# Moving operands of the 256-token stages at one column, and transposes between the passes of the last two feed-forwards

## What is computed

```
h = x + 0.5 * swiglu(rmsnorm(x, ffn1_norm[l]), gate, up, down)   # 1024 -> 2816 -> 1024
u = rmsnorm(h, mix_norm[l])
h = h + (pool_mixer(u) if l == 0 else mla_attention(u, shared k and v))
h = h + 0.5 * swiglu(rmsnorm(h, ffn2_norm[l]), gate, up, down)
out = rmsnorm(h, final_norm)[:, 16:]

swiglu(h) = (silu(h @ w_gate) * (h @ w_up)) @ w_down
```

## Time and profile before

| | |
|---|---|
| median of three runs | 1222.82 us |
| profiled execution | 1223.91 us |
| its span | 1222.4 us |
| TensorE busy | 1201.7 us (98%), 9978 matmuls |
| VectorE busy | 859.5 us (70%) |
| ScalarE busy | 635.1 us (52%) |
| GpSimd busy | 174.1 us (14%) |

### The profile page before, as it was taken

One profiled execution on the slowest core, in us unless ns is written; L12 is line 12 of the kernel. 1 busy time (PEld: TensorE's weight loads), 2 busy tenths in 40 slices (PEclk: granted clock), 3 DMA queues, 4 the chain that ended last, 5 costly groups with the idle time before them and its releaser, 6 DMA issues.

```text
span 1222.4 us, 23818 instructions
## 1 busy us (share of the span) xinstructions
PE 1201.7 (98%) x9978; PEld 1179.0 (96%) x9978; DVE 859.5 (70%) x1215; ACT 635.1 (52%) x990; POOL 174.1 (14%) x178
## 2 busy tenths in 40 slices
PE   6999999999999999999999999999999999999998
PEld 4999989999999999999999999999999998999998
DVE  6789888776666866655766666667666787766653
ACT  5657646665445444543644444444545457645532
POOL 3025324000322000022200001230001231000021
PEclk9999999999999999999999999999999999999999
DMA  9897765757564555654355565456556532665550
GB/s 363 312 349 265 241 241 181 257 203 282 161 222 151 175 186 182 196 176 142 118 181 184 184 193 174 155 180 197 193 187 210 191 121 87 206 187 194 189 174 35
DMA packets 67051, 239.17 MB, mean 196 GB/s; under 512 B 7380, under 2 KB 8549, under 8 KB 66944
## 3 DMA queue, kind: packets, MB, share of 16 engines
q1 hardware_dynamic: 66144, 235.15, 57.9%
q0 software_dynamic: 656, 2.24, 0.5%
q10 hardware_dynamic: 144, 0.26, 0.1%
HBM read 236.55 MB, written 1.07 MB: 194 GB/s over the span
## 4 chain that ended last, share of the span: by engine, by line
PE 91%; DVE 3%; ACT 1%; issue 0%; DVEq 0%
PE G L636 27%; PE G L637 27%; PE G L638 27%; DVE sb_wlo L1624 1%; PE A L636 1%; PE A L637 1%; PE A L638 1%; PE A L788 0%; PE A L1082 0%; PE A L803 0%; PE A L776 0%; PE G L1137 0%; PE G L1138 0%; PE G L1139 0%; DVE sb_rstd L1672 0%
## 5 line engine op out<-in xcount | busy, mean ns | idle before, releaser
L1624 DVE TENSOR_TENSOR sb_wlo<-sb_raw,sb_whi 128x1024 fp32r<-128x1024 f32 (+1 forms) x398 | 488.1, 1260 | 76.9 <-ACT sb_whi L1217 76.7
L636 PE MATMUL G<-sb_xh,sb_whi 128*128 128x256 f32 (+2 forms) x1752 | 495.7, 283 | 0.9 <-DVE sb_wlo L1624 0.8
L1217 ACT ACTIVATE sb_whi<-sb_raw 128x1024 fp32r<-128x1024 f32 (+1 forms) x397 | 404.4, 1044 | 173.8 <-PE G L638 154.9
L637 PE MATMUL G<-sb_xl,sb_whi 128*128 128x256 f32 (+2 forms) x1752 | 493.9, 282 | 0.0
L638 PE MATMUL G<-sb_xh,sb_wlo 128*128 128x256 f32 (+2 forms) x1752 | 493.4, 282 | 0.0
L636 PEld LDWEIGHTS G<-sb_xh,sb_whi 128*128 128x128 f32 x1752 | 329.5, 188 | 1.5 <-DVE sb_wlo L1624 1.3
L637 PEld LDWEIGHTS G<-sb_xl,sb_whi 128*128 128x128 f32 x1752 | 329.7, 188 | 0.0
L638 PEld LDWEIGHTS G<-sb_xh,sb_wlo 128*128 128x128 f32 x1752 | 329.6, 188 | 0.0
L636 PE MATMUL G<-sb_hh,sb_whi 128*128 128x256 f32 (+1 forms) x1041 | 292.3, 281 | 1.5 <-DVE sb_hh L1866 1.4
L638 PE MATMUL G<-sb_hh,sb_wlo 128*128 128x256 f32 (+1 forms) x1041 | 291.5, 280 | 0.0
L637 PE MATMUL G<-sb_hl,sb_whi 128*128 128x256 f32 (+1 forms) x977 | 273.5, 280 | 0.0
(11 more groups left out here) (352 smaller groups left out, 1254.4 us busy)
## 6 DMA issues: line engine op xcount, KB each, us to landing
sb_raw<-in_wstream SPq DMA_DIRECT2D x438, 512.0 KB, 4.4
sb_raw<-in_wstream SPq DMA_DIRECT2D x8, 320.0 KB, 7.6
sb_bias<-bias_scratch POOLq DMA_DIRECT2D x1, 2048.0 KB, 16.5
sb_X<-in_xT SPq DMA_DIRECT2D x2, 512.0 KB, 5.1
out_tok<-sb_y SPq DMA_DIRECT2D x3, 256.0 KB, 3.1
sb_con<-in_consts SPq DMA_DIRECT2D x1, 601.0 KB, 10.0
sb_band<-in_bands SPq DMA_DIRECT2D x1, 314.0 KB, 4.1
out_tok<-sb_y ACTq DMA_DIRECT2D x1, 256.0 KB, 3.3
```

What stands on the lines that cost most here:

```text
L636: e.matmul(out, w_h, xs, start=k0 + s.kt == 0, stop=False)
L637: e.matmul(out, w_h, xr, start=False, stop=False)
L1217: e.activation(whi[:, i % NSPLIT, 0:w], raw[:, c % NRAW, 0:w], ACT.Copy).then_inc(hi_done, 1)
L1624: e.tensor_tensor(wlo[:, i % NSPLIT, 0:w], raw[:, c % NRAW, 0:w], f(whi[:, i % NSPLIT, 0:w]), ALU.subtract).then_inc(lo_done, 1)
```

## The change

The begin columns of `walk` become 16 for all eight row tiles. And `swiglu` gets a parameter: so many transposes of a piece of the constants into the bank A3, ahead of tile 2, ahead of tile 12, and ahead of the first and the third part of the down product. Their result is read by nobody. The third feed-forward gets one at each of the four places, the fourth gets four at each.

```diff
-        walk = (32, 48, 0) + 5 * (META,)
+        walk = KT * (META,)
...
+            def settle(n):
+                for _ in range(n):
+                    e.transpose(A[3][:, 0:P], con[:, 16:16 + P], ident)
+
-            def swiglu(f_, means, each=None, order=None, between=None):
+            def swiglu(f_, means, each=None, order=None, between=None, settled=0):
...
                 for j in range(2, FF2):
+                    if j in (2, 12):
+                        settle(settled)
                     if between and j == 4:
                         between()
...
                 for i in range(4):
+                    if i % 2 == 0:
+                        settle(settled)
+
...
-            swiglu("ffn1_1", {16: latent_mean})
+            swiglu("ffn1_1", {16: latent_mean}, settled=1)
...
-            swiglu("ffn2_1", {21: ffn2_1_mean})
+            swiglu("ffn2_1", {21: ffn2_1_mean}, settled=4)
```

## The result

The changed kernel takes 1227.74 us (median of six runs, 1226.95 to 1228.14), the kernel before 1222.79 beside it (six runs, 1222.50 to 1224.02): a ratio of 1.0039 with a 95% interval of 1.0028 to 1.0049. It is slower by 4.95 us, and lies above the range. The profiled executions differ by 4.2 us (1223.91 and 1228.14), their spans by 4.3.

The account below looks back on a forecast made before the run. TensorE, 98% busy, was taken as the bound: number of matmuls times the distance of starts. Passes -3.52, query projection -0.14 and transposes +2.44 made -1.2 us: median 1221.6 us, range 1219.6 to 1226.0.

Parts of the forecast that it names:

- the knock: In each feed-forward pass, a row at column 0 or 32 knocks the stream out of the slow pace; the change removes it.
- I take quick at all eight places: Behind all eight places of transposes in both feed-forwards the stream goes on at the quick pace, 113.3 ns per matmul.
- Rows and projection, -3.66: Column 16 at the quick pace gains 3.52 us in both feed-forwards' passes and 0.14 in the query projection.
- Transposes, +2.44: Added TensorE time: four places of one transpose, 0.60 us, and four places of four, 1.84 us.
- First passes and stage h at nothing: Feed-forwards' first passes taken as 0, with 0.4 us either way; first stage as 0, between 1.9 gain and 1.3 loss.
- They can't gain, and lose 2.4 us if slow.: Down products behind the passes, 528 matmuls in each feed-forward, are quick already; slow, they lose 2.4 us.
- One place fails: Rival: one place leaves half the passes slow (+0.9 us, 1223.7) or half the downs (0.0, 1222.8); chance 0.17.
- The single transpose doesn't free the stream: Rival: third feed-forward stays slow at passes 2 and 12, 1225.9 us, or 1227 to 1228 with down products; chance 0.15.
- The first stage turns quick: Rival: stage h, without rows at 0 and 32, gains 1.6 us of the 1.9, so -2.8, 1220.0; chance 0.13.
- The paces don't depend on the rows: Rival: the change only adds transposes, +2.4 us, 1225.2; chance 0.05.

Follow-up runs that it names:

- once_four: Changed kernel with four transposes ahead of tile 2 in each feed-forward and none at the other places; 1220.24 us, ratio 0.9975.
- transposes_only: Changed kernel with the old begin columns (32, 48, 0, then 16) put back and the transposes kept; 1227.39 us, ratio 1.0038.
- rows_only: Changed kernel without its transposes in either feed-forward, column 16 kept for all row tiles; 1232.39 us, ratio 1.0076.

## Why the prediction was wrong

The two paces, their sizes and the part that the rows play were right: passes at column 16 alone are even, at 113.3 or 117.8 ns, and the knock is gone. What fell is the step "**I take quick at all eight places**". Four of the eight came out slow, and the query projection behind one of them:

```
third, tiles 2 to 11             480 matmuls
third, down products, both       528
query projection                  72
fourth, tiles 12 to 21           480
together                        1560 x 4.5 ns = 7.0 us
```

- *Rows and projection, -3.66.* Right as prices of a quick stream: once_four, with two places, came out 0.2 us from what they give. Two of four halves of the passes had them.
- *Transposes, +2.44.* Four measured 0.44 where I took 0.46, one 0.11 where I took 0.15: 0.2 us less in all.
- *First passes and stage h at nothing.* Right in size. Both first passes stay slow behind their mean; ahead of it, the third's turned quick (48 matmuls, 0.2 us). The branch products behind stage h start at 142.17 us instead of 142.21, but that is luck, as is shown below the list.
- *"They can't gain, and lose 2.4 us if slow."* The down products were the place that I weighed least. They had come quick out of the passes, and a place in front of a quick stream can only lose. I had read the transposes as a cure, and asked only whether they free a slow stream. They start it anew, and a new start has its own draw.
- *One place fails* (0.17) priced one place; four failed. *The single transpose doesn't free the stream* (0.15), priced at 1225.9 to 1228, has the right time by a mechanism that is half right: a single one left the stream slow at tile 2 but freed it at tile 12, and then threw it back at the down products; and a group of four failed at tile 12 of the fourth. *The first stage turns quick* is right in direction and far too large at 1.6 us. *The paces don't depend on the rows* is refuted by transposes_only, whose passes are uneven again.
- The rows that I had, three and four transposes with quick streams and seven with a slow one, were three draws. That none of these streams was slow before its transposes holds for the four alone: ahead of the three, 22 distances from 102.02 to 104.61 took 2.59 us, 117.7 ns each, and ahead of the seven, from 110.07 to 112.66, as long; only in their last row tile, the one at column 16, do they turn quick (116, 114, 113 ns). The change was to have long slow streams ahead of the first place. A choice of the same outcome at eight places was more than they could carry.

The gates of stage h did turn quicker. Their modelled mean was 279 ns before, between the quick stream's 276 and the slow one's 281, and is 277 now (L637 of the changed kernel, gates by shape, 77 to 142 us):

```profile
L637 PE MATMUL G<-sb_xl,sb_whi 128*128 128x256 f32 x128 | 35.5, 277 | 0.0
```

By starts they take 64.11 us (from 78.06) instead of 64.55 (from 77.66), and the stretch ahead of them, which has waits, took as much more. In all twelve profiles with rows at column 16 the gates take 64.10 to 64.40 us, in the two with the old columns 64.55 and 64.74. From 24 to 142 us the twelve take 117.12 to 118.14 us, 117.5 on average, and the two 118.13 and 118.15. So column 16 was worth some 0.6 us there, by an estimate from these profiles (there are only two with the old columns), and that of the changed kernel shows the least of it.

The sum with the 1560: -1.2 + 7.0 = +5.8 in the span, and 4.3 was measured. Of the 1.5, 0.7 is the out projection, which was slow in the profile before and quick in the profile after (155 products from 174.31 us, a draw behind a wait), 0.2 a start of tile 2 that is earlier still, 0.2 the cheaper transposes, and 0.2 the wait at 953.88, which a slower TensorE no longer meets; 0.2 is left over. The medians differ by 4.95 us, more than the profiled executions do by 0.7; draws behind waits, which change between executions, are of that size, but no run shows that they are the cause.

Two questions stay open: what the state is that a stream keeps, and why the draw at tile 2 repeats in every profile while that behind the mean splits into two groups. A kernel with another number of transposes also has every later instruction at another position in its program; no run holds the two apart. A place in a quick stream is a risk and no certainty: the down products of the fourth feed-forward stayed quick at both of theirs in transposes_only. The 272-column stages weren't tried.

## What to carry to other kernels

Price a stream of matmuls by the distance of its starts, and look at its pace before and behind every interruption: a stream may keep a slower pace, at full clock and with no wait, until something breaks it. A remedy that restarts a stream is to be put once, where the stream is slow, and looked up in the trace of that very kernel; each further one is a new draw and can undo the first (four places in each feed-forward, 1227.7 us; one, with four transposes, 1220.2). And take several runs of the winner: a place that splits into two groups, 13.5 us apart, can look like a gain in a single profile.

## What the runs showed of the hardware

Matmuls of 256 columns with a weight load each run at 113.3 or at 117.8 ns under one granted clock of 1.00, and stayed in one pace for 1535 matmuls, 181 us, in rows_only. A place of transposes ahead of a tile or of a part of the down product has a draw that came out the same in both profiles of the changed kernel. Over 24 places it goes, with one transpose, in a cycle of three (slow, quick, slow); with two, three and four it is quick at all places behind the first or second, in one execution each. Behind waits the draw changes between executions of one kernel. None of this goes with DMA traffic: 0.02 and 0.62 of DMA share stand beside the quick pace, 0.06 and 0.61 beside the slow one.
